# Scores' bias, scale and maximum in one VectorE operation, and the last norm's root without Pool's power

## The reference, cut to what matters

```python
# branch A: sliding window of 128, 8 heads, one learned sink for each head
sc = where(valid, q @ k.T * 64 ** -0.5 + bias, -inf)      # 128 queries x 256 keys
m = maximum(max(sc), sink);  e = exp(sc - m)
p = e / (sum(e) + exp(sink - m))
# branch B: 4 heads, two maps each, causal over all keys up to the query's block
sc = where(dist >= 0, q @ k.T * 64 ** -0.5 + bias, -inf)  # 128 queries x up to 512 keys
a = softmax(sc[0]) - lam * softmax(sc[1])
# the end: y is the experts' sum of a token
x = x + gt_f * (y * rsqrt(mean(y * y) + eps) * g)
```

## Time and profile before

| what | us |
|---|---|
| median of 3 runs | 1726.31 |
| lowest, highest | 1725.14, 1730.0 |
| the profiled execution, its own time | 1730.17 |
| its span, first to last instruction | 1728.0 |
| TensorE busy in the span | 1647.2 |
| VectorE busy | 1372.0 |
| ScalarE busy | 1097.9 |
| Pool busy | 202.4 |

### The profile page before, as it was taken

The page is one execution under the profiler, slowest core; times in us unless marked ns, Lnnn a source line. Parts: engine busy times, 40 slices in busy tenths (PEclk is TensorE's granted clock), DMA queues, the critical chain, the costliest instruction groups (busy, mean ns, idle before and its releaser), DMA issues.

```text
span 1728.0 us, 19602 instructions
## 1 busy us (share of the span) xinstructions
PE 1647.2 (95%) x7482; PEld 1294.2 (75%) x7482; DVE 1372.0 (79%) x1017; ACT 1097.9 (64%) x903; POOL 202.4 (12%) x156
## 2 busy tenths in 40 slices
PE   8999987798799999999999999999999999999994
PEld 3888865544578888888888888888888888888883
DVE  5564459655688989899888988899898988899894
ACT  3322237622567777777777777777777777777772
POOL 2200000204101000110001000110001000111112
PEclk9999998897799999999999999999999999999997
DMA  9866530124899999999999999999999999999964
GB/s 343 240 228 201 184 119 1 41 85 147 298 407 388 373 383 386 388 355 385 383 381 368 371 379 387 388 367 384 380 378 377 367 388 389 379 354 374 385 233 159
DMA packets 156725, 540.93 MB, mean 313 GB/s; under 512 B 13980, under 2 KB 15112, under 8 KB 156515
## 3 DMA queue, kind: packets, MB, share of 16 engines
q1 hardware_dynamic: 140880, 500.20, 76.1%
q0 software_dynamic: 13648, 35.26, 8.5%
q10 hardware_dynamic: 2100, 4.21, 0.7%
HBM read 522.94 MB, written 29.66 MB: 320 GB/s over the span
## 4 chain that ended last, share of the span: by engine, by line
PE 88%; DVE 4%; DMA 3%; issue 2%; POOL 1%; ACT 1%; POOLq 0%; SPq 0%; ACTq 0%; DVEq 0%
PE ps L1130 66%; PE ps L1104 4%; PE ps L1639 3%; PE ps L1640 3%; PE ps L661 3%; PE ps L1641 3%; PE ps L1120 2%; DMA oh<-const_buckets 1%; DMA raw<-in_w_ada 1%; POOL slot_rows L957 1%; DVE st L517 1%; DMA expert_sums<-yb,icur 0%; DMA xb<-h_ffn,stab 0%; DVE st L499 0%; DVE s_sb L496 0%
## 5 line engine op out<-in xcount | busy, mean ns | idle before, releaser
L1248 DVE TENSOR_TENSOR wl<-rawm,wh 128x2048 fp32r<-128x2048 f32 x420 | 947.0, 2288 | 147.0 <-ACT wh L1177 142.6
L1177 ACT ACTIVATE wh<-rawm 128x2048 fp32r<-128x2048 f32 x420 | 802.1, 1919 | 260.3 <-PE ps L1130 260.3
L1130 PE MATMUL ps<-wh,xh 128*128 128x512 f32 x1120 | 360.6, 403 | 3.5 <-DVE xl L1261 3.5
L1130 PE MATMUL ps<-wl,xh 128*128 128x512 f32 x1120 | 346.2, 390 | 0.0
L1130 PE MATMUL ps<-wh,xl 128*128 128x512 f32 x1120 | 346.0, 390 | 0.0
L1130 PEld LDWEIGHTS ps<-wh,xh 128*128 128x128 f32 x1120 | 211.3, 189 | 53.2 <-DVE xl L1261 4.9
L1130 PEld LDWEIGHTS ps<-wl,xh 128*128 128x128 f32 x1120 | 211.3, 189 | 45.0
L1130 PEld LDWEIGHTS ps<-wh,xl 128*128 128x128 f32 x1120 | 210.8, 188 | 44.3
L1130 PE MATMUL ps<-wh,ah 128*128 128x512 f32 x560 | 179.8, 402 | 2.5 <-DVE al L1265 2.5
L1130 PE MATMUL ps<-wl,ah 128*128 128x512 f32 x560 | 173.8, 392 | 0.0
L1130 PE MATMUL ps<-wh,al 128*128 128x512 f32 x560 | 173.0, 390 | 0.0
(11 more groups left out here) (256 smaller groups left out, 1588.8 us busy)
## 6 DMA issues: line engine op xcount, KB each, us to landing
rawm<-in_w_gate_up SPq DMA_DIRECT2D x280, 1024.0 KB, 9.8
rawm<-in_w_down SPq DMA_DIRECT2D x140, 1024.0 KB, 7.8
raw<-in_w_ada SPq DMA_DIRECT2D x20, 1024.0 KB, 6.2
raw<-in_w_in SPq DMA_DIRECT2D x16, 1024.0 KB, 5.2
rawx<-in_w_ada SPq DMA_DIRECT2D x4, 1024.0 KB, 15.5
wo<-in_w_out SPq DMA_DIRECT2D x2, 2048.0 KB, 12.2
bias_vectors_repeated<-bias_vectors POOLq DMA_DIRECT2D x1, 2304.0 KB, 13.5
xs<-in_x ACTq DMA_DIRECT2D x1, 2048.0 KB, 12.9
```

Of the source, the lines that this page charges most:

```text
L1130: ins = nc.tensor.matmul(banks[:, n, :], left[:, kk, :], right[:, k, n * UN:(n + 1) * UN], start=begins and kk == 0 and i == 0, stop=kk == ...
L1177: nc.scalar.activation(flat(wh[v % SPL][:]), flat(rawm[v][:]), ACT.Copy).then_inc(wh_done, 1)
L1248: nc.vector.tensor_tensor(flat(wl[v][:]), flat(rawm[v][:]), flat(wh[v % SPL][:]), ALU.subtract).then_inc(wl_done, 1)
```

## The change

The bias is stored divided by the scale (L1802 and a new `farbs`). In an A unit the maximum starts from the sink. In a B unit with far keys the near part's maximum starts from the far part's. `s_ready` is counted once for a unit, when the last of them is through. In the last norm VectorE's reciprocal and ScalarE's square root stand for Pool's power; a square root is done once ahead of the loop.

```diff
             if kind == "A":
                 lo = P if n == 0 else 0
-                nc.vector.scalar_tensor_tensor(dst, src, QK_SCALE, toep[:, 4 * g:4 * g + 4, lo:2 * P], ALU.mult,
-                                               ALU.add).then_inc(s_ready, 1)
-                dve.wait_ge(s_ready, total(n_scores, i))
-                nc.vector.tensor_reduce(st[:, w, MX, :], dst, AX_X, ALU.max).then_inc(mx_step, 1)
-                dve.wait_ge(mx_step, total(n_max, i) - 2)
-                nc.vector.scalar_tensor_tensor(st[:, w, NMX, :], st[:, w, MX, :], -1.0, nsink[:, 4 * g:4 * g + 4],
-                                               ALU.mult, ALU.min).then_inc(mx_step, 1)
+                for h in range(4):
+                    ins = nc.vector.tensor_tensor_reduce(dst[:, h, :], src[:, h, :], toep[:, 4 * g + h, lo:2 * P], QK_SCALE,
+                                                         sinkb[:, 4 * g + h:4 * g + h + 1], ALU.add, ALU.max,
+                                                         st[:, w, MX, h:h + 1])
+                ins.then_inc(s_ready, 1)
+                dve.wait_ge(s_ready, i + 1)
+                nc.vector.tensor_scalar(st[:, w, NMX, :], st[:, w, MX, :], -1.0, None, ALU.mult).then_inc(mx_step, 1)
...
             if near:
-                nc.vector.tensor_scalar(dst[:, :, 0:near], src[:, :, 0:near], QK_SCALE, farb[:, g:g + 1], ALU.mult,
-                                        ALU.add).then_inc(s_ready, 1)
-            dve.wait_ge(s_ready, total(n_scores, i))
-            nc.vector.tensor_reduce(st[:, w, MX, 0:2], dst, AX_X, ALU.max).then_inc(mx_step, 1)
+                for m in range(2):
+                    nc.vector.tensor_tensor_reduce(dst[:, m, 0:near], src[:, m, 0:near],
+                                                   farbs[:, g:g + 1].to_broadcast([P, near]), QK_SCALE, LOWEST, ALU.add,
+                                                   ALU.max, st[:, w, FMX, m:m + 1]).then_inc(far_step, 1)
+            for m in range(2):
+                if near:
+                    dve.wait_ge(far_step, total(n_far, i) - 1 + m)
+                ins = nc.vector.tensor_tensor_reduce(dst[:, m, near:near + width], src[:, m, near:near + width],
+                                                     toep[:, H_A + g, 2 * P - width:2 * P], QK_SCALE,
+                                                     st[:, w, FMX, m:m + 1] if near else LOWEST, ALU.add, ALU.max,
+                                                     st[:, w, MX, m:m + 1])
+            ins.then_inc(s_ready, 1)
...
-    def final_pool(pool, power):
-        for t in range(TC):
-            power(rs1[:, 2, t:t + 1], rs1[:, 1, t:t + 1], frs_step, 2 * t + 1)
...
+            dve.wait_ge(frs_step, 3 * t + 1)
+            nc.vector.reciprocal(rs1[:, 2, t:t + 1], rs1[:, 1, t:t + 1]).then_inc(frs_step, 1)
             nc.vector.tensor_tensor(yo[:, t, :], yo[:, t, :], gpf[:], ALU.mult).then_inc(fg_ready, 1)
...
     def final_act(act):
+        nc.scalar.activation(warm[:], one[:], ACT.Sqrt).then_inc(warmed, 1)
...
+            act.wait_ge(frs_step, 3 * t + 2)
+            nc.scalar.activation(rs1[:, 2, t:t + 1], rs1[:, 2, t:t + 1], ACT.Sqrt).then_inc(frs_step, 1)
```

More of the change, by code:

```diff
@@ L222, in program @@
     sinkb = small("sinkb", [P, H_A], F32)
-    nsink = small("nsink", [P, H_A], F32)
     farb = small("farb", [P, H_B], F32)
+    farbs = small("farbs", [P, H_B], F32)
     subg = small("subg", [P, 1], F32)
@@ L243, in program @@
     st = at("st", [P, IN_FLIGHT, 8, 4], F32, 35 * KB)
-    NMX, MX, DSK, ESK, SUM, DEN, FAC = range(7)
+    NMX, MX, DSK, ESK, SUM, DEN, FAC, FMX = range(8)
+    LOWEST = -3e38
     sn = at("sn", [P, 3, H_B], F32, 35 * KB + 512)
@@ L310, in program @@
               "o_ready"))
+    far_step = sem("far_step")
     osq_ready, sn_ready, on_ready, ot_ps, ot_ready = map(
@@ L360, in total, with n_far @@
         return sum(count(u) for u in UNITS[:i + 1])
-    def n_scores(u):
-        return 2 if u[0] == "B" and u[1] >= 2 else 1
+    def n_far(u):
+        return 2 if u[0] == "B" and u[1] >= 2 else 0
     def n_max(u):
-        return 3 if u[0] == "A" else 2
+        return 2 if u[0] == "A" else 1
     def n_exp(u):
@@ L404, in scores @@
             if i >= 2:
-                pe.wait_ge(s_ready, total(n_scores, i - 2))
+                pe.wait_ge(s_ready, i - 1)
             if kind == "A":
@@ L508, in before @@
             width = (n + 1) * P - near
-            tile = toep[:, H_A + g:H_A + g + 1, 2 * P - width:2 * P].to_broadcast([P, 2, width])
-            nc.vector.scalar_tensor_tensor(dst[:, :, near:near + width], src[:, :, near:near + width], QK_SCALE, tile,
-                                           ALU.mult, ALU.add).then_inc(s_ready, 1)
             if near:
-                nc.vector.tensor_scalar(dst[:, :, 0:near], src[:, :, 0:near], QK_SCALE, farb[:, g:g + 1], ALU.mult,
-                                        ALU.add).then_inc(s_ready, 1)
-            dve.wait_ge(s_ready, total(n_scores, i))
-            nc.vector.tensor_reduce(st[:, w, MX, 0:2], dst, AX_X, ALU.max).then_inc(mx_step, 1)
-            dve.wait_ge(mx_step, total(n_max, i) - 1)
+                for m in range(2):
[10 more added lines that the diff above has]
+            ins.then_inc(s_ready, 1)
+            dve.wait_ge(s_ready, i + 1)
             nc.vector.tensor_scalar(st[:, w, NMX, 0:2], st[:, w, MX, 0:2], -1.0, None, ALU.mult).then_inc(mx_step, 1)
@@ L1401, in finished @@
             dve.wait_ge(fg_ready, t + 1)
-            dve.wait_ge(frs_step, 2 * t + 2)
+            dve.wait_ge(frs_step, 3 * t + 3)
             nc.vector.scalar_tensor_tensor(x1e[:, t, :], yo[:, t, :], rs1[:, 2, t:t + 1], x1e[:, t, :], ALU.mult,
@@ L1801, in _ @@
             dve.wait_ge(rv_ps, b + 1)
-            nc.vector.tensor_copy(rv[0:n, b, :], ps[0:n, 6 + b, 0:REL]).then_inc(rv_ready, 1)
+            nc.vector.tensor_scalar(rv[0:n, b, :], ps[0:n, 6 + b, 0:REL], 1.0 / QK_SCALE, None, ALU.mult).then_inc(rv_ready, 1)
         dve.wait_ge(small_in, 16 * N_SMALL)
@@ L1807, in _ @@
         nc.vector.tensor_scalar(subgs[:], subg[:], 1.0 - LAM_INIT, None, ALU.mult).then_inc(lam_step, 1)
-        nc.vector.tensor_scalar(nsink[:], sinkb[:], -1.0, None, ALU.mult).then_inc(lam_step, 1)
+        nc.vector.tensor_scalar(farbs[:], farb[:], 1.0 / QK_SCALE, None, ALU.mult).then_inc(lam_step, 1)
         dve.wait_ge(bada_in, 16)
@@ L1917, in _ @@
         experts_pool(pool)
-        final_pool(pool, power)
 _INS = ['x', 'c', 'rel_bias_table', 'w_ada', 'b_ada', 'g_mix_pre', 'g_mix_post', 'g_ffn_pre', 'g_ffn_post', 'w_in',
```

## The result

| | before | after |
|---|---|---|
| median of 6 runs each on one chip, us | 1729.58 | 1709.77 |
| lowest, highest | 1725.14, 1730.4 | 1708.6, 1712.21 |
| profiled execution, own time | 1730.17 | 1710.79 |
| its span | 1728.0 | 1709.0 |

What follows compares the result with a forecast made beforehand. VectorE was taken to set the pace in attention's tiles 1 to 3. Blocks -9.3 us, less 2.1 lost at joins, norm +0.3, gave -6.9 us: median 1726.31 becomes 1719.4, range 1713.5 to 1728.5.

Steps and rivals of the forecast that it cites:

- The bottleneck: Attention, tiles 1 to 3: VectorE sets the pace, TensorE second with 4.2 to 6.8 us to spare in a tile.
- the price of the read: VectorE's score blocks: getting each maximum out adds 0.08 us per operation, so blocks save 9.3 us rather than 14.4.
- costs no instruction: Rival, score blocks: the maximum needs no instruction, each operation is 0.08 us less, net -10.8 us, 1715.5; chance 0.16.
- The clock rival: TensorE gets its clock back: 2.1 us at joins not lost, some 3 us go at the end, -12.0, 1714.3; chance 0.10.
- The objection raised against the rival: Against TensorE regaining its clock: before attention's last piece it would still idle while it waits for the norm.
- The joins: Starts of tiles 1 and 3, where another engine follows VectorE: 1.4 and 0.7 us of the block savings are lost.
- Tile 0: Attention's first tile: blocks hardly change and VectorE does not set its stretch; taken as nothing, 1 us to either side.
- The norm: Last norm: reciprocal adds 0.2 us in each of tiles 0 to 2, tile 3 gains 0.3; together +0.3 us.
- Pool's queue loses four waits that nothing stood behind: Last norm: taking Pool's powers out removes four waits from its queue, with nothing behind them; no gain counted.
- Half rate: Rival, new operation: two cycles per element, 0.27 us more per 256 elements, +7.0 us, 1733.3, slower; chance 0.07.
- The rule on half throughput: Skill's rule: the form with a scalar and two SBUF sources that are not bf16 runs at half throughput; L541 contradicts it.
- Two of the signs of being wrong: Attention: TensorE waiting for `s_ready` before scores, and VectorE idle more than 2 us in total in tiles 1 to 3.

Runs made afterwards that it cites:

- e4: The changed kernel with an unread maximum added in each block, sized to give blocks their old length on VectorE: 1724.51 us, ratio 0.9971 to the kernel before.
- e10: The kernel before with the new operation in the B units alone, A units and last norm unchanged: 1718.98 us, ratio 0.9952.
- e5: The kernel before with the one-hot table's load put ahead of the two gain rows on Pool's queue: 1725.78 us, ratio 0.9984.
- e2: The kernel before with the new last norm alone: 1723.82 us, ratio 0.9975.
- e12: The changed kernel with the one-hot table's load put ahead of the two gain rows, nothing else: 1709.00 us, ratio 0.9892 to the kernel before.
- e6: The kernel before with Pool's power in the last norm for tiles 0 to 2, reciprocal and square root for tile 3: 1723.39 us, ratio 0.9971.

## Why the prediction was wrong

**The bottleneck was read rightly.** VectorE set the pace in tiles 1 to 3, what its blocks lost arrived but for tile 1's join, and the merge and experts behind it kept their length (+0.6, where the other profiles scatter from 1364.4 to 1367.2). e4 shows it in the one direction, tiles 2 and 3 of e10 with a second dose.

**The step that failed is the price of the read: "I take 0.08, since ops without a wait between them do overlap on this engine".** The reason given was sound and was not applied to the read itself: in the earlier trace rows an operation of 0.48 us is followed after 0.40, and the read starts just where the next operation would. Measured: 0.08 long, 0.00 on the path. Over 64 operations that is 5.1 us, and the blocks save 14.1 rather than 9.3. The Trainium skill ("VectorE: DVE Perf Modes", section on two Vector instructions with no wait between them) says that there are two instructions, and the trace agrees; that it adds a read's length to the sum was my inference. The rival "costs no instruction" had the right sum, for a wrong reason, at 0.16.

**The second step that failed: the rivals were taken as exclusive.** The free read came together with a faster TensorE in the tail. The clock rival at 0.10 expected no loss at the joins and some 3 us in the last stretch; measured were a loss of 1.9 in tile 1, 0.2 in tile 2, none in tile 3, and 2.1 us less in the tail. The tail's part is TensorE's clock (0.74 to 0.89), and e4, with the blocks long again, has 12.54 us at 0.78. In tiles 2 and 3 the clock rose too, but there it gave nothing that can be seen: with the old blocks tile 2 takes 22.01 us at 1.00 (e5) and 22.02 at 0.84 (e2). The objection raised against the rival came true, TensorE still idles 3.79 us before the last piece, and yet did not decide it, because the pieces ahead of that wait got shorter (1.91 to 1.06 for eight).

**The joins** were forecast to lose 1.4 in tile 1 and 0.7 in tile 3. Tile 1 lost 1.9, three B blocks at the place named, as a B block there gave 0.64 rather than 0.48; tile 3 nothing, and why it lost nothing was not tested. Tile 0 was put at nothing: its blocks shortened by 2 x 0.23 + 4 x 0.37 = 1.9, and its stretch by 0.2, in a tile that scatters by 1.8 between profiles of the same blocks; whether anything of it arrives is open.

**The norm** was right term by term: +0.29 for +0.3, the root under L1402, one hidden table load. It was wrong in the sentence "Pool's queue loses four waits that nothing stood behind": the program's end stood behind Pool, for 3.0 us. The row for it, Pool's drain at L91, is in the trace of before, behind the last operation on data.

**The start**, -2.4 in the profile, was no term of the sum. e5 and e12 show that it is the wait for one late table, with the slower products behind it. That this change removed it is luck: no term of the forecast leads to it, and what links the two is open.

**Half rate** did not happen: 256 elements of the new operation follow each other after 0.40 us, 128 after 0.27 (244.09 - 243.82), so 128 more are 0.13, as for L541. The rule on half throughput that the prediction weighed from the Trainium skill ("Vector Engine (DVE) Microarchitecture Reference") can't be tested by this operation, whose one source is in PSUM; L541, which has both in SBUF, goes against it with the same 0.13.

**Two of the signs of being wrong** told nothing. TensorE did wait for `s_ready` before scores (L418 for L499, 2.9 us), but it had done so before (L416 for L496, 2.4 us). VectorE was idle for more than 2 us in tiles 1 to 3 of after (4.4 by the windows), but also in before (3.2).

With the measured terms the sum is: blocks -14.1, joins +2.1, tile 0 -0.2, tail -2.1, norm +0.3, end -3.0, start -2.4, the rest +0.6, together -18.8 for the 19.0 measured.

## What to carry to other kernels

Price a new operation by the distance from one start to the next, with its second instruction laid over that distance, and ask of each rival whether it can hold together with the forecast. Compare two profiles stretch by stretch, and know each stretch's scatter first: a total can agree with a theory whose mechanism did not happen, as in e10. Where an engine is taken out of the last stage, read the rows of the program's end too: an engine whose last operation comes late can hold the end by its drain. And when several parts of a change each give something, time each part by itself: over a quarter of the span gained here, 5.4 of 19.0 us, lay outside attention and the last norm, at the start and the end of the program.

## What the runs showed that was not expected

- An operation of VectorE that also gives its maximum reads it out with an instruction 0.08 us long that runs beside the next operation: 0.40 us from start to start with it, 0.40 for L541 without.
- Pool's drain at the program's end lasts until 7.2 us after its last power, in before (1727.7 for 1720.5) and in e6 (1721.9 for 1714.7). It costs time only when that is later than the output's landing.
- One more instruction on ScalarE around 1700 us goes with a software queue's transfer at 46 us landing 0.5 to 1.5 us sooner, in seven kernels of seven. The cause is open.
- TensorE's granted clock did not set the length of tiles 2 and 3: with the old blocks tile 2 took 22.01 to 22.04 us at granted clocks from 0.84 to 1.00. In the tail it did: 13.24 us at 0.74 (before), 11.14 at 0.89 (after), 10.74 at 1.00 (e10).
- A wait of 1.3 us of TensorE for one small table cost 2.4 us, since the products behind it followed each other after 0.43 rather than 0.23 us for 3.75 us.
